# A decoder step with a mixture of experts: the router rewritten, a memset moved, identity products added

## What is computed

```
z  = rmsnorm(x) @ w_in                      # 1024 x 5120
m  = sigmoid(gate_a) * rglru(conv4(xa)) + sigmoid(gate_b) * (silu(layernorm(conv31(v))) @ w_pw + b)
h  = x + m @ w_out
xf = rmsnorm(h)
logits = xf @ w_router + b_router           # 32 experts
vals, idx = top_k(logits, 4); combine = softmax(vals) spread over 32 columns
for e in range(32):
    g = min(xf @ w_gate[e] + b_gate[e], 7); u = clip(xf @ w_up[e] + b_up[e], -7, 7)
    out += combine[:, e] * (((u + 1) * g * sigmoid(1.702 * g)) @ w_down[e] + b_down[e])
y  = rmsnorm(h + out) * g_final
```

## Time and profile before

| what | value |
| --- | --- |
| median of three executions | 1195.98 us |
| the profiled execution | 1196.15 us, span 1194.4 us |
| PE busy / weight loads | 1110.8 us (93%) / 509.0 us |
| DVE, ACT, POOL busy | 429.0, 166.4, 90.6 us |
| moved by transfers | 440.38 MB, mean 369 GB/s |
| chain that ended last | PE 70%, DMA 27% |

### The profile page before, as it was taken

How to read it: one execution, slowest core, us unless ns; L and a number is a source line. 1 busy time by engine, 2 the same in 40 slices (tenths; PEclk the granted TensorE clock), 3 DMA queues, 4 the chain that set the end, 5 groups by cost and what they waited for, 6 DMA issues and landing times.

```text
span 1194.4 us, 15234 instructions
## 1 busy us (share of the span) xinstructions
PE 1110.8 (93%) x5769; PEld 509.0 (43%) x5770; DVE 429.0 (36%) x1012; ACT 166.4 (14%) x329; POOL 90.6 (8%) x124
## 2 busy tenths in 40 slices
PE   6999999989999989899999898999999999999896
PEld 5777777654433324233433232333333333333333
DVE  4899999442132313131222222222222121212123
ACT  3211156230010010101000000000000000000103
POOL 3565220130000000000000000000000000000000
PEclk9999999989999999999999999999999999999999
DMA  9973433559999999999999999999999999999995
GB/s 285 318 232 135 152 136 109 212 193 374 427 428 426 426 429 427 427 427 427 427 429 430 427 427 429 430 429 427 427 429 430 428 428 428 429 430 427 429 427 191
DMA packets 59298, 440.38 MB, mean 369 GB/s; under 512 B 4983, under 2 KB 27767, under 8 KB 34795
## 3 DMA queue, kind: packets, MB, share of 16 engines
q1 hardware_dynamic: 58042, 436.94, 89.2%
q0 software_dynamic: 1024, 2.77, 0.8%
q10 hardware_dynamic: 192, 0.14, 0.0%
HBM read 438.24 MB, written 2.43 MB: 369 GB/s over the span
## 4 chain that ended last, share of the span: by engine, by line
PE 70%; DMA 27%; DVE 1%; ACT 1%; issue 0%; SPq 0%; DVEq 0%
PE ps L1149 26%; DMA ring<-in_w_gate 24%; PE ps L941 13%; PE ps L1209 11%; PE ps L1239 4%; PE ps L1128 4%; PE ps L1029 3%; PE ps L1052 2%; DMA ring<-in_w_down 2%; PE ps L909 2%; PE ps L1141 1%; PE ps L1243 1%; PE ps L1019 1%; PE ps L1334 1%; PE ps L1130 1%; PE ps L1202 1%
## 5 line engine op out<-in xcount | busy, mean ns | idle before, releaser
L1149 PE MATMUL ps<-ring,ws 128*64 128x512 f32 x2032 | 460.6, 598 | 40.7 <-DMA ring<-in_w_up 24.5
L1149 PEld LDWEIGHTS ps<-ring,ws 128*64 128x64 f32 x2032 | 139.6, 137 | 329.8 <-issue 247.8
L1209 PE MATMUL ps<-ring,ws 128*64 128x512 f32 x960 | 216.7, 595 | 6.9 <-DMA ring<-in_w_down 6.9
L941 PE MATMUL ps<-ws,ring 128*128 128x288 f32 x640 | 158.6, 410 | 0.0
L941 PEld LDWEIGHTS ps<-ws,ring 128*128 128x128 f32 x640 | 122.7, 192 | 34.2
L1209 PEld LDWEIGHTS ps<-ring,ws 128*64 128x64 f32 x960 | 65.7, 137 | 125.5 <-issue 105.5
L1712 DVE TENSOR_TENSOR acc<-ps,acc 128x1024 f32<-128x1024 f32 x30 | 36.8, 1225 | 191.6 <-PE ps L1239 191.6
L1689 DVE TENSOR_SCALAR ws<-ps 128x512 f32<-128x512 f32 x32 | 22.1, 692 | 197.2 <-PE ps L1149 197.2
L1508 DVE SCALAR_TENSOR_TENSOR ps<-ws,par,ps 128x256 f32<-128x256 f32 x232 | 91.8, 483 | 0.2 <-DVE ps L1508 0.2
L1694 DVE TENSOR_SCALAR ws<-ps 128x512 f32<-128x512 f32 x32 | 22.1, 692 | 159.5 <-PE ps L1149 159.5
L813 ACT COPY ws<-ps 64x512 f32<-64x512 f32 x62 | 35.9, 579 | 257.8 <-PE ps L1209 257.5
(11 more groups left out here) (228 smaller groups left out, 699.0 us busy)
## 6 DMA issues: line engine op xcount, KB each, us to landing
ring<-in_w_up SPq DMA_DIRECT2D x64, 2048.0 KB, 25.0
ring<-in_w_gate SPq DMA_DIRECT2D x63, 2048.0 KB, 24.9
ring<-in_w_down SPq DMA_DIRECT2D x60, 2048.0 KB, 23.7
ring<-in_w_in SPq DMA_DIRECT2D x20, 1024.0 KB, 13.4
ring<-in_w_conf_pw SPq DMA_DIRECT2D x4, 1024.0 KB, 6.0
ring<-in_w_out SPq DMA_DIRECT2D x4, 1024.0 KB, 6.1
ring<-in_w_down SPq DMA_DIRECT2D x4, 1024.0 KB, 22.7
ws<-in_w_gate SPq DMA_DIRECT2D x2, 1024.0 KB, 16.4
```

What stands on the lines that cost most here:

```text
L941: ins = nc.tensor.matmul(z[:, 0:T], w[:, k, i * P:(i + 1) * P], hn[:, k, :], start=(k == 0), stop=(k == NT - 1))
L1149: ins = nc.tensor.matmul(ps[h * CAP:(h + 1) * CAP, bk + q // 2, :], x_e[:, KQ * (q % 2) + t, b, :], w[:, t, h * 512:(h + 1) * 512], start= ...
L1209: ins = nc.tensor.matmul(ps[h * CAP:(h + 1) * CAP, bk, :], hid_t[:, b, k % KQ, k // KQ, :], w[:, h * 512:(h + 1) * 512], start=False, stop ...
```

## The change

- The memset of `bias` on GpSimd now waits until VectorE has emptied the filling hn7.
- The order of jobs is out01, logits2, turn 0 (a, b), out10, logits0, ht1a, out11, ht1b, logits1. The rows are turned unscaled from `acc`; the factor of the norm comes in at `choose`, the gain g_ffn is multiplied into the router's weights once. `take_turned` is a plain copy. Half of tile 1 is turned in the middle of out11, and its logits are taken in two halves. The sample rows are repeated in acc (`repeat_samples`) before they are turned.
- Before `complete(2)` VectorE waits for all three stores (s_store), as h_rest overlays st_h.
- The subtractions for the three bf16 parts go from GpSimd to VectorE (`rest`, `low`), ScalarE makes two of the parts instead of three. For tile 1 they come behind the first gather.
- Experts 0 and 1 are gathered together: `sel_inv` holds 0/1 times the factor of the norm in fp32, `gather_first` multiplies it with `acc` (24 products with 128 columns) into two banks. The second gather behind expert 0's chunks goes.
- slot_no begins at 1, so that the step that took 1 off the ranks goes; mask in fp32 and its extra steps go; the ranks of the sample tile use 32 rows and a repeated triangle `tri_s`.
- SyncE loads the fourth early row block ahead of the second ring chunk, and the 2 MB of `spare` when the scan is done; h_tok takes up 4096 words, so that spare no longer overlays h_cm.
- `keep_warm(z, n)` issues n fp32 products of the identity with itself (128 columns): 3 behind out11, 3 behind the last half turn, 6 ahead of the ranks, 5 ahead of the first gather, 17 in all.

The diff, cut to its core:

```diff
-    jobs += [(n, "v") for n in ("out2", "out00", "ht2a", "ht2b", "out01", "logits2", "out10", "ht0a", "ht0b", "out11",
-                                "logits0", "ht1a", "ht1b", "logits1", "rank")]
+    jobs += [(n, "v") for n in ("out2", "out00", "ht2a", "ht2b", "out01", "logits2", "ht0a", "ht0b", "out10", "logits0",
+                                "ht1a", "out11", "ht1b", "logits1", "rank")]
...
-        h_tok = take(TILES * D).rearrange("p (i d) -> p i d", i=TILES)
+        h_tok = take(SLOT)[:, 0:TILES * D].rearrange("p (i d) -> p i d", i=TILES)
...
+        h_rest = hid_t_w[:, 0:D]
+        sel_inv = sel_w
...
                 for k in range(2):
-                    sp.dma_start(early_down[k], w_down[EARLY, k // KQ, :, k % KQ * D:(k % KQ + 1) * D]).then_inc(s_early, 16)
+                    load_early(k)
+                sp.wait_ge(s_st, N_ST)
+                load_early(3)
                 load_gu(0, 2)
+                sp.wait_ge(filled, JOB["gb7"] + 1)
+                sp.wait_ge(s_hs, 1)
+                for h in range(2):
+                    sp.dma_start(spare[:, h * HALF:(h + 1) * HALF],
+                                 w_down[EARLY, 1, :, h * HALF:(h + 1) * HALF]).then_inc(s_early, 16)
                 load_gu(0, 3)
                 load_gu(1, 0)
...
-                def load_early(k):
-                    sp.dma_start(early_down[k], w_down[EARLY, k // KQ, :, k % KQ * D:(k % KQ + 1) * D]).then_inc(s_early, 16)
-                sp.wait_ge(s_st, N_ST)
-                load_early(3)
                 sp.wait_ge(filled, JOB["logits1"] + 1)
                 load_early(2)
-                sp.wait_ge(s_split, 3 * TILES)
-                for h in range(2):
-                    sp.dma_start(spare[:, h * HALF:(h + 1) * HALF],
-                                 w_down[EARLY, 1, :, h * HALF:(h + 1) * HALF]).then_inc(s_early, 16)
                 load_gu(1, 3)
...
+                pool.wait_ge(empt_v, EV("hn7"))
                 pool.memset(bias[:, :, :], 0.0)
...
-                def rest(n, i):
-                    pool.wait_ge(filled, JOB[f"ht{i}b"] + 1)
-                    for s in range(2):
-                        pool.wait_ge(s_split, 3 * n + s + 1)
...
-                        pool.tensor_tensor(h, h, part, ALU.subtract).then_inc(s_rest, 1)
-                pool.wait_ge(s_m, NT)
-                for n, i in enumerate(TILE_ORDER):
-                    rest(n, i)
...
+                def h_part(n, i, s):
...
+                    if s == 0:
+                        act.wait_ge(s_hn, n + 1)
+                        ins = act.activation(part, acc[0:rows, i, :], ACT.Copy, scale=stat[0:rows, 21 + i:22 + i])
+                    else:
+                        act.wait_ge(s_rest, n + 1)
+                        ins = act.copy(part, h_rest[0:rows, :])
+                    ins.then_inc(s_split, 1)
+                for n, i in enumerate((2, 0)):
+                    if i == 2:
+                        act.wait_ge(s_rep, 1)
+                    else:
+                        act.wait_ge(empt_v, EV("out01"))
+                    square(i, y_e, 12)
                     root(i, TILES + n + 1, 15)
-                    act.wait_ge(s_hn, n + 1)
-                    for s in range(3):
-                        if s:
-                            act.wait_ge(s_rest, 2 * n + s)
...
-                        act.copy(part, h_tok[0:rows, i, :]).then_inc(s_split, 1)
+                    for s in range(2):
+                        h_part(n, i, s)
+                act.wait_ge(empt_v, EV("out10"))
+                act.activation(y_e[:, 0:512], acc[:, 1, 0:512], ACT.Square, accum_out=stat[:, 9:10])
+                act.wait_ge(empt_v, EV("out11"))
+                act.activation(y_e[:, 512:D], acc[:, 1, 512:D], ACT.Square, accum_out=stat[:, 13:14]).then_inc(s_sq, 1)
+                act.wait_ge(s_ms, 2 * TILES)
+                act.activation(stat[:, 19:20], stat[:, 16:17], ACT.Sqrt, scale=1.0 / D).then_inc(s_root, 1)
+                for s in range(2):
+                    h_part(2, 1, s)
...
+                def keep_warm(z, n):
+                    for _ in range(n):
+                        nc.tensor.matmul(z[:, 0:P], ident[:], ident[:], start=True, stop=True)
+                def turn_h(i, h, ready):
+                    pe.wait_ge(*ready)
+                    z = fill(f"ht{i}{'ab'[h]}")
+                    for k in range(4):
+                        ins = turn(z[:, k * P:(k + 1) * P], acc[:, i, cols(4 * h + k)])
+                    ins.then_inc(filled, 1)
...
                 out_rows(0, (0,))
-                turn_h(2)
+                for h in range(2):
+                    turn_h(2, h, (s_rep, 1))
                 out_rows(0, (1,))
                 logits(2)
+                for h in range(2):
+                    turn_h(0, h, (empt_v, EV(f"out0{h}")))
                 out_rows(1, (0,))
-                turn_h(0)
-                out_rows(1, (1,))
                 logits(0)
-                turn_h(1)
-                logits(1)
+                fill("ht1a")
+                z = fill("out11")
+                for k in range(NT):
+                    if k == NT // 2:
+                        turn_h(1, 0, (empt_v, EV("out10")))
+                    ins = nc.tensor.matmul(z[:, :], mt[:, k, P:2 * P], w_out_cols(k, 1), start=(k == 0), stop=(k == NT - 1))
+                ins.then_inc(filled, 1)
+                keep_warm(fill("ht1b"), 3)
+                z = fill("logits1")
+                logits_half(1, 0, z)
+                turn_h(1, 1, (empt_v, EV("out11")))
+                keep_warm(fill("rank"), 3)
+                logits_half(1, 1, z).then_inc(filled, 1)
                 z = fill("rank")
+                keep_warm(z, 6)
                 pe.wait_ge(s_mask, TILES)
                 for i in range(TILES + 1):
                     for j in range(min(i + 1, TILES)):
...
                 ins.then_inc(filled, 1)
+                def gather_first(z, ts):
+                    for n, t in enumerate(ts):
+                        for i in range(TILES):
+                            rows = P if i < 2 else T_S
+                            ins = nc.tensor.matmul(z[:, n * 2 * CAP:(n + 1) * 2 * CAP], acc[0:rows, i, cols(t)],
+                                                   sel_inv[0:rows, i].rearrange("p b s -> p (b s)"),
+                                                   start=(i == 0), stop=(i == TILES - 1))
+                    return ins
...
-                pe.wait_ge(s_split, 3 * TILES)
                 pe.wait_ge(s_btab, 3)
-                pe.wait_ge(s_zrow, 1)
-                gather(0, 0)
+                keep_warm(ps[:, BK_X, :], 5)
+                pe.wait_ge(s_selp, TILES)
+                for h, bk in ((1, BK_X), (0, BK_SEL)):
+                    gather_first(ps[:, bk, :], range(4 * h, 4 * h + 4)).then_inc(s_xg, 1)
                 pe.wait_ge(empt_v, EV("rank"))
...
                 for m in range(2):
                     gate_up_bias(0, 0, m)
                 pe.wait_ge(s_xe, 1)
-                for q in range(1, 4):
+                gate_up_chunk(0, 1, slots[0], fills[0], last=False)
+                pe.wait_ge(s_xe, 2)
+                for q in range(2, 4):
                     gate_up_chunk(0, q, slots[q - 1], fills[q - 1], last=(q == 3))
-                gather(1, 1)
                 for m in range(2):
                     gate_up_bias(1, 1, m, BK_OUT)
-                pe.wait_ge(s_xe, 2)
                 gate_up_chunk(1, 0, slots[3], fills[3], BK_OUT)
...
+                def repeat_samples():
+                    dve.wait_ge(empt_v, EV("out2"))
+                    for r in range(1, 3):
+                        ins = V.tensor_copy(acc[r * T_S:(r + 1) * T_S, 2, :], acc[0:T_S, 2, :])
+                    ins.then_inc(s_rep, 1)
+                def h_factor(n, i):
+                    dve.wait_ge(s_root, TILES + n + 2)
+                    V.reciprocal(stat[:, 21 + i:22 + i], stat[:, 18 + i:19 + i]).then_inc(s_hn, 1)
+                def take_turned(i, h):
+                    z = full(f"ht{i}{'ab'[h]}")[:, :].rearrange("p (k t) -> p k t", k=4)
+                    V.tensor_copy(h_cm[:, 4 * h:4 * h + 4, i * P:(i + 1) * P], z).then_inc(empt_v, 1)
...
+                def rest(n, i):
+                    dve.wait_ge(s_split, 2 * n + 1)
...
+                    V.scalar_tensor_tensor(h_rest[0:rows, :], acc[0:rows, i, :], stat[0:rows, 21 + i:22 + i], high, ALU.mult,
+                                           ALU.subtract).then_inc(s_rest, 1)
+                def low(n, i):
+                    dve.wait_ge(s_split, 2 * n + 2)
...
+                    V.tensor_tensor(part, h_rest[0:rows, :], mid, ALU.subtract).then_inc(s_low, 1)
+                def choose(n, i):
+                    dve.wait_ge(s_hn, n + 1)
+                    V.scalar_tensor_tensor(lg[:, i, 0:E], full(f"logits{i}")[:, 0:E], stat[:, 21 + i:22 + i], b_rt[:], ALU.mult,
+                                           ALU.add).then_inc(empt_v, 1)
```

(58 more changed lines are left out.)

97 lines of the change are left out of this document (40 added, 57 removed).

## The result

| | before | after |
| --- | --- | --- |
| median of five runs each | 1196.58 us | 1203.24 us |
| lowest and highest | 1195.93, 1197.93 | 1202.49, 1203.35 |
| profiled execution (span) | 1196.15 (1194.4) | 1203.33 (1201.6) |
| next ring chunk issued | 274.99 | 283.91 |
| span minus that time | 919.4 | 917.7 |

The ratio after to before is 1.0054, with an interval of 1.0043 to 1.0065: slower, by 6.7 us, where a gain of 5.9 us was forecast. The table's last two lines already hold the place of the loss. The end still lies a fixed time behind the issue of the first ring chunk that has to wait for a slot. This fixed time became 1.7 us shorter, as the hole closed; the issue came 8.9 us later.

A forecast was written before the change was run, and what follows sets the result against it. Transfer engines are full from 300 us on, so the end moves only with the full stream's beginning and its holes. Terms -2.3 - 2.6 (holding the +1.6) - 1.0 = -5.9 from 1196.15 gave 1190.2 us, range 1188.3 to 1194.5.

The forecast's parts named there:

- the hole: Transfer stretch at 320 GB/s in 296 to 300 us, where a slot came free too late; forecast to close, worth 1.0 us.
- What bounds the kernel: Transfer engines are full from 300 us on; the end moves only by when the full stream begins and holes in it.
- Head: At the start, moving GpSimd's memset ends its contention with VectorE; all 2.3 us reach the router: -2.3.
- Moved loads: 2 MB of early down rows move to behind the scan, where transfer engines idle in 203 to 210: costs nothing.
- Store wait: Before the router VectorE waits for all three stores, the last landing at 228.3; TensorE stalls by +1.6 us.
- The rival with 236: A store lands at about 236 instead of 228.3, stalling TensorE before the router: +3.5, 1199.5 us; chance 0.05.
- Router up to the gather: On the old clock, before subtracting 2.3: logits1 complete at 262.1, gather starting at 265.4; an identity product 0.13 us.
- Gather: First gather's 24 fp32 products at 0.107 us each take 2.8 us with a tail; bounds 2.6 to 5.1.
- Behind the gather: The second gather goes, slots come free sooner and the 1.0 us gap in the transfer stream closes: -1.0.
- Half clock: Identity products fail to hold TensorE's clock in router and gather: up to +6.1, 1196.2 us, middle 1194.7; chance 0.13.
- The slower rival: VectorE waits for a store landing behind the chunks issued at 218 and 219, stalling TensorE: 1199.5 us; chance 0.05.

The follow-up runs named there:

- e6: e4 with the second half of the first gather put behind expert 0's first chunk, the early row still queued ahead of the first slot's chunk; 1198.48 us.
- e11: e9 with the second half of the first gather behind the first chunk and the early row's load queued behind the first slot's chunk; 1191.22 us.
- e5: The changed kernel with the wait before GpSimd's memset taken out, so that it runs at the start as before; 1205.57 us.
- e4: The changed kernel with h rows copied by ScalarE into chunk order, so the gather's weights are adjacent; g_final and one early row loaded after the gather; 1195.08 us.
- e8: e4 without VectorE's wait for the stores, h_rest moved to y_e and the squares' unused output to x_e; 1193.47 us.
- e1: The changed kernel with 128 neighbouring channels as weights of the first gather instead of every fourth (wrong channels, same work); 1194.93 us.
- e2: The changed kernel with every second channel as weights of the first gather (wrong channels, same work); 1196.02 us in one execution.
- e9: e8 with the first gather made of 32 bf16 products for tiles 0 and 2 and 8 fp32 products for tile 1; 1188.62 us.
- e3: The changed kernel without its 17 identity products; 1204.11 us.
- e7: e4 without the 17 identity products; 1202.48 us.
- e12: e8 without the six identity products in the two short waits, 3 behind out11 and 3 behind the last half turn; 1194.54 us.
- e13: e9 without any of the 17 identity products; 1191.4 us.

## Why the prediction was wrong

**What bounds the kernel** held. Span minus the issue of the first slot's chunk is 917.5 to 918.1 in the changed kernel and in ten of the twelve variants; the exceptions are the two split ones, e6 (920.2) and e11 (920.6). The time moves with that issue and with nothing later.

**Head** (-2.3): right. 2.33 by the medians of e5 and the changed kernel; the memset has 6.3 us to spare in its new place.

**Moved loads** (0): right, by the stretch 203 to 210.

**Store wait** (+1.6): the mechanism was right, and 1.6 lie between e4 and e8. The changed kernel's own profile shows less, 0.87 us of idle time: the store landed 6.7 us after its issue, where 7.3 had been taken from rows 5. The rival with 236 did not come.

**Router up to the gather**: logits1 complete at 258.96, forecast 262.1 - 2.3 = 259.8; gather begun at 262.73, forecast 265.4 - 2.3 = 263.1. The subtractions on VectorE held nothing up: in 228 to 254 TensorE is busy for 25.73 of 26 us. An identity product took 0.24 and not 0.13 (six are the x12 of 1.42 us in the chain), since it too is two instructions. I had priced it from the bare pace of single instructions. Most lie in waits, so this cost under a microsecond.

**Gather** (2.8, bounds 2.6 to 5.1; measured 15.5): this step failed, and the term was wrong in four ways. "24 fp32 products at 0.107" took the projections' pace of 0.2425, which is that of one instruction, scaled it to 128 columns, and multiplied it by the number of products in the code. Each fp32 product is two load and product pairs, and the row for L1071 showed it: x16 for eight products. The pace itself was right as long as the number of rows stays the same (0.11 measured). The changes between 128 and 32 rows, the spacing of the weights and the clock's fall were not in the term. The working apart, by runs and traces:

- forecast 24 x 0.107 with a tail: 2.8
- the count: 48 pairs at 0.11 with a tail make 5.5, so +2.7
- 15 changes between 128 and 32 rows at 0.2: +3.0. This makes the 8.5 measured in e1 and e4. With the right count my own two prices, 0.107 and 0.21, would have bounded it by 5.1 and 10.1
- the spacing of four words: 18 pairs took 5.13 us at clock 1.00, 0.285 each, so 13.7 for 48: +5.2
- the clock at 0.50 from 267.86 on: +1.8 in the gather (30 pairs at 0.345), and behind it biases 1.00 instead of the forecast's 0.5, and 4.7 us instead of 3.7 from the start of the first chunk to the issue of the next ring chunk: +1.5

In the gather these make 2.7 + 3.0 + 5.2 + 1.8 = 12.7, with what lies behind it 14.2; less 0.4 for the gather's earlier start and 0.7 for the hole (below), 13.1. The profiled executions differ by 1203.33 - 1196.15 = +7.2 where -5.9 was forecast: 13.1.

**Behind the gather** (-1.0): the mechanism was right, the hole closed; 919.4 became 917.7, so it was -1.7.

**The rivals.** Half clock came true, but for another reason than the one weighed. I looked at idle time, and there was hardly any: the fall at 267.86 came in the midst of 15.5 us of unbroken work, and TensorE had not paused since 262.73. The price I set, 2.8 for the gather, hung on the wrong gather. The slower rival forecast a loss, but by another mechanism, the stores; that the kernel became slower does not bear it out. A rival on the added work's own price was missing, though the text said itself that nothing in the trace of before showed such a product; the range was drawn from 2.6 to 5.1 as if it did.

**What stays open.** Why the clock falls in the changed gather and not in e1, e2 and e4. The changed kernel, e1 and e2 differ by the weights' spacing alone, so the slow loads bring it about, but no run shows by which measure. Nor is a spacing of three words or of more than four measured, nor a gather with the number of rows as the only difference, nor e9 with places for g_final and the early row that need not wait for the gather.

## What to carry to other kernels

Count instructions and not products when a new operation is priced: take the xN of a row of the same type, and let the upper bound be set by load and product one after the other. Look in the trace whether the loads follow one another without a gap; here each change between weights of 128 and of 32 rows cost 0.2 us. Look at the stride with which weights are read; laying the rows out once on an idle engine gained here 8.2 us (1203.24 to 1195.08), and using parts that exist in bf16, with 128 rows in every piece, another 4.9 (e8 to e9). Filler products pay by what runs at half clock without them, so shorten that first; and before work is moved ahead of a queue's next transfer, see which bytes used the idle time before.

## What the runs showed of the hardware

- At a granted clock of 1.00 an fp32 weight load of 128x128 takes 190 ns from adjacent words (e1), 195 from every second (e2), and 324 from every fourth (the changed kernel). bf16 loads four elements apart took 114 (e9).
- At 0.50 the spaced load still takes 324 (e3), and the adjacent one as long (e7):

```profile
L1157 PEld LDWEIGHTS ps<-ws 128*128 128x128 f32 x32 | 7.4, 322 | 3.7 <-issue 3.7
```

- At 2.4 GHz pairs of fp32 load and product with 128 columns and adjacent weights follow one another every 0.11 us, and every 0.31 where the number of weight rows changes between 128 and 32 (e1, e4, e8). The mean of this gather is 0.177 (8.51/48), at 1.2 GHz 0.313 (15.03/48, e7); with spaced weights 0.285 and 0.345 (10.34 us for the 30 pairs that are left), or 0.333 where all are at 1.2 GHz (e3).
- The clock can fall behind one pause of 0.88 us among short products (e12, e13) and under unbroken slow loads (the changed kernel), and it came back in e12 within 3.2 us of products and short loads, where in e7 it stayed down for 20.4.
